# Shifting rows by DMA within SBUF instead of by matrix products, a regrouped long convolution, and a split tail, in a two-layer diffusion trunk

## The reference

```python
u = xm @ w_in                                   # 3584 columns and 16 gate columns
def short_conv3(x, w):                          # along the 128 tokens, on 1536 columns
    xp = jnp.pad(x, ((0, 0), (1, 1), (0, 0)))
    return xp[:, :L] * w[0] + xp[:, 1:L + 1] * w[1] + xp[:, 2:] * w[2]
v, x1, x2 = jnp.split(short_conv3(u[..., :1536], conv_w), 3, axis=-1)
z = x1 * (long_conv(v, h[0]) + d[0] * v)        # long_conv: by Fourier transform, length 256
z = x2 * (long_conv(z, h[1]) + d[1] * z)
...                                             # beside it: bidirectional mLSTM on q, k, v, gates
out = sum over 8 experts e of gates[:, e] * swiglu(x, w1[e], w3[e], w2[e])
x = x + g2 * out                                # the two outputs of 128 x 1024
```

## Time and profile before

| what | value |
|---|---|
| median of 3 runs | 1426.8 us (1423.72 to 1427.9) |
| the profiled execution: its own time | 1426.66 us |
| its span, first to last instruction | 1424.8 us |
| mean granted TensorE clock | 0.979 of full speed |
| busy: PE, DVE, ACT, POOL | 1352.3, 1040.3, 811.0, 29.6 us |
| the mixer's stretch with the short convolution | about 134 to 192 us |
| start of the mixer's output projection on PE | 251.87 us |
| expert stage | about 590 to 1411 us |
| last instruction of DVE | 1419.56 to 1420.25 us |

### The profile page before, as it was taken

The page is one execution under the profiler, slowest core; times in us unless marked ns, Lnnn a source line. Parts: engine busy times, 40 slices in busy tenths (PEclk is TensorE's granted clock), DMA queues, the critical chain, the costliest instruction groups (busy, mean ns, idle before and its releaser), DMA issues.

```text
span 1424.8 us, 16335 instructions
## 1 busy us (share of the span) xinstructions
PE 1352.3 (95%) x6382; PEld 1052.3 (74%) x6382; DVE 1040.3 (73%) x1008; ACT 811.0 (57%) x893; POOL 29.6 (2%) x52
## 2 busy tenths in 40 slices
PE   5889998999999988999999999999999999999994
PEld 1566564778888777788888888888888888888883
DVE  0446447754544685578898898998988988989885
ACT  1343212444334556467777777777777777777672
POOL 3000000000000200000000000000000000000000
PEclk9799999999999999999999999999999999999997
DMA  9899958765555522459999999999999999999990
GB/s 328 310 330 336 328 199 295 191 214 195 183 177 187 175 74 90 148 187 363 365 355 351 340 347 363 366 348 337 349 339 366 366 345 342 347 363 364 345 336 32
DMA packets 289348, 405.17 MB, mean 284 GB/s; under 512 B 16117, under 2 KB 224272, under 8 KB 289200
## 3 DMA queue, kind: packets, MB, share of 16 engines
q1 hardware_dynamic: 282048, 391.23, 80.4%
q0 software_dynamic: 2944, 8.47, 1.9%
q10 hardware_dynamic: 4272, 4.34, 0.9%
HBM read 402.12 MB, written 1.87 MB: 284 GB/s over the span
## 4 chain that ended last, share of the span: by engine, by line
PE 87%; DVE 5%; ACT 3%; DMA 3%; issue 1%; SPq 1%; DVEq 0%
PE bank L1773 84%; DMA raw<-in_w_ada 2%; PE bank L2140 2%; DVE w_lo L506 1%; DMA raw<-in_ev_w_in 1%; ACT arena L1044 1%; SPq L607 1%; ACT w_hi L499 1%; DVE Gb L1211 0%; PE bank L1829 0%; ACT xn L795 0%; DVE x_lo L1219 0%; PE bank L2237 0%; PE bank L2271 0%; DVE arena L1763 0%
## 5 line engine op out<-in xcount | busy, mean ns | idle before, releaser
L506 DVE TENSOR_TENSOR w_lo<-raw,w_hi 128x2048 fp32r<-128x2048 f32 (+1 forms) x238 | 543.3, 2284 | 157.2 <-ACT w_hi L499 155.5
L499 ACT CAST w_hi<-raw 128x2048 fp32r<-128x2048 f32 (+1 forms) x238 | 451.8, 1899 | 138.4 <-PE bank L1773 85.1
L1773 PE MATMUL bank<-w_hi,x_hi 128*128 128x512 f32 x1072 | 433.8, 405 | 6.3 <-DVE x_lo L1219 1.7
L1773 PE MATMUL bank<-w_lo,x_hi 128*128 128x512 f32 x1072 | 422.6, 394 | 0.0
L1773 PE MATMUL bank<-w_hi,x_lo 128*128 128x512 f32 x1072 | 419.9, 392 | 0.0
L1773 PEld LDWEIGHTS bank<-w_hi,x_hi 128*128 128x128 f32 x1072 | 202.0, 188 | 55.3 <-issue 9.5
L1773 PEld LDWEIGHTS bank<-w_hi,x_lo 128*128 128x128 f32 x1072 | 202.3, 189 | 46.5
L1773 PEld LDWEIGHTS bank<-w_lo,x_hi 128*128 128x128 f32 x1072 | 202.5, 189 | 38.6 <-issue 0.2
L506 DVE TENSOR_TENSOR w_lo<-arena,w_hi 128x2048 fp32r<-128x2048 f32 x88 | 201.7, 2292 | 36.3 <-ACT w_hi L499 36.3
L499 ACT CAST w_hi<-arena 128x2048 fp32r<-128x2048 f32 x88 | 168.0, 1910 | 28.0 <-PE bank L1773 28.0
L1773 PE MATMUL bank<-w_hi,g_hi 128*128 128x512 f32 x440 | 174.1, 396 | 1.8 <-DVE g_lo L1487 1.8
(11 more groups left out here) (281 smaller groups left out, 923.3 us busy)
## 6 DMA issues: line engine op xcount, KB each, us to landing
raw<-in_moe_w SPq DMA_DIRECT2D x352, 512.0 KB, 5.5
arena<-in_moe_w SPq DMA_DIRECT2D x176, 512.0 KB, 5.4
raw<-in_w_ada SPq DMA_DIRECT2D x96, 512.0 KB, 6.9
raw<-in_ff_w SPq DMA_DIRECT2D x66, 512.0 KB, 4.4
raw<-in_ev_w_in SPq DMA_DIRECT2D x28, 512.0 KB, 8.5
raw<-in_at_w_qkv SPq DMA_DIRECT2D x12, 512.0 KB, 4.4
raw<-in_ev_w_out SPq DMA_DIRECT2D x8, 512.0 KB, 6.3
Gb<-gate_rows POOLq DMA_DIRECT2D x8, 512.0 KB, 4.5
```

The lines of the kernel that those rows point to most:

```text
L499: nc.scalar.copy(w_hi[:, t % SPL, c], place[:, c]).then_inc(hi_ok, 1)
L506: nc.vector.tensor_tensor(w_lo[:, t % SPL, c], raw_slot(n)[0][:, c], w_hi[:, t % SPL, c].bitcast(F32), ALU.subtract).then_inc(lo_ok, 1)
L1773: return pe.matmul(out, lhsT, rhs, start=start, stop=stop)
```

## The change

- The short convolution uses no matrix products. ACT issues, for each block of 512 columns, two DMAs within SBUF: `u`'s rows 0 to 126 go to rows 1 to 127 of `earlier`, rows 1 to 127 to rows 0 to 126 of `later`, for both `g` at once. DVE's `short_conv(c)` waits until both have landed and then makes three products and two sums. POOL zeroes the two edge rows once, which it waits for ahead of its DMA of the taps.
- The mixer's order is changed on PE, ACT and DVE: all `weight_logs` come before pair 11, `fft(0)` to `inverse_fft(3)` lie between `mixer_half(11, 1)` and `ada(23)` and each comes one or two pieces earlier than before. Two blocks of the convolution's DMAs wait for `cv_ok`, in ACT's own order.
- In every expert's last chunk `down` finishes bank 4 before bank 5, with a semaphore between them, and ACT and DVE split each half by itself. The last expert's `combine` goes by halves of the columns, into four banks. POOL prepares `x` and the factor ahead of it, so that DVE makes one product and one sum for each quarter, and ACT issues four stores, each when its quarter is ready, before the flag is read.

```diff
-        ztmp = hyT0[:, 2, :]
+        ztmp = xn[:, 1, 0:HW]
+        earlier, later = hyT0[:, 0:2, :], hyT0[:, 2:4, :]
...
@@ gpsimd
+            pool.wait_ge(f_nrm, 2)
+            gp.memset(earlier[0:1], 0.0).then_inc(sh_z, 1)
+            gp.memset(later[96:P], 0.0).then_inc(sh_z, 1)
             for w in range(3):
                 if w:
                     pool.wait_ge(cv_ok, 2 * w)
...
+            pool.wait_ge(cb_t, 4 * (NE - 1))
+            last_gate = rw[:, 68:88].rearrange("p (g e) -> p g e", g=G)[:, :, NE:NE + 1]
+            for q in range(4):
+                g, c = q // 2, slice(512 * (q % 2), 512 * (q % 2) + 512)
+                chained(gp.tensor_tensor(stage[:], acc[:, g, c], Gb[:, g, c], ALU.mult))
+                chained(gp.tensor_tensor(x[:, g, c], x[:, g, c], stage[:], ALU.add))
+                chained(gp.tensor_scalar(acc[:, g, c], Gb[:, g, c], last_gate[:, g, :], None, ALU.mult))
+                pool.sem_inc(x_sum, 1)
@@ scalar
+            def shift_rows(w):
+
+                if w == 0:
+                    eng.wait_ge(sh_z, 2)
+                else:
+                    eng.wait_ge(cv_ok, 2 * w)
+                eng.wait_ge(tj_t, 7 + 2 * w + 2)
+                uw = u[:, :, HW * w:HW * w + HW]
+                eng.dma_start(earlier[1:P], uw[0:P - 1]).then_inc(sh_l, 16)
+                eng.dma_start(later[0:P - 1], uw[1:P]).then_inc(sh_l, 16)
...
             take_pair(7, block_of(u, 0))
+            shift_rows(0)
             high(IN[10])
             take_spectra(4)
             take_spectra(5)
             high(IN[11])
-            take_pair(9, block_of(u, HW))
-            high(IN[12])
             weights(0)
             weights(1)
+            take_pair(9, block_of(u, HW))
+            shift_rows(1)
+            high(IN[12])
+            weights(2)
+            weights(3)
             high(IN[13])
             take_pair(11, block_of(u, 2 * HW))
+            shift_rows(2)
             high(IN[14])
-            weights(2)
-            weights(3)
...
+            def store(r):
+
+                for i in range(2):
+                    c = slice(512 * i, 512 * i + 512)
+                    for g, name in enumerate(("y_prompt", "y_sample")):
+                        eng.wait_ge(fin, 4 * r + 2 * i + g + 1)
+                        eng.dma_start(o[name][0][:, c], x[:, g, c]).then_inc(stored, 16)
@@ vector
+            def short_conv(c):
 
                 w, g = c // 2, c % 2
+                uc, before, after = u[:, g, HW * w:HW * w + HW], earlier[:, g, :], later[:, g, :]
                 eng.wait_ge(ld_cw, 16 * (w + 1))
+                eng.wait_ge(sh_l, 32 * (w + 1))
+                v_.tensor_tensor(before, before, convw[:, 0, :], ALU.mult)
                 link(v_.tensor_tensor(uc, uc, convw[:, 1, :], ALU.mult))
+                v_.tensor_tensor(after, after, convw[:, 2, :], ALU.mult)
+                link(v_.tensor_tensor(uc, uc, before, ALU.add))
+                v_.tensor_tensor(uc, uc, after, ALU.add).then_inc(cv_ok, 1)
...
             low(IN[9])
             low(IN[10])
+            short_conv(0)
+            short_conv(1)
             low(IN[11])
             weighted(0)
             weighted(1)
+            low(IN[12])
+            short_conv(2)
+            short_conv(3)
             weighted(2)
             weighted(3)
+            low(IN[13])
...
             fft_product(0)
+            low(IN[14])
+            short_conv(4)
+            hyena_gate(0)
+            short_conv(5)
@@ tensor, from pair 9 on (new order)
             mixer_half(9, 0)
             ada(14)
             weight_logs(0)
             weight_logs(1)
             mixer_half(9, 1)
             ada(15)
+            eng.wait_ge(wt_ok, 1)
+            weight_logs(2)
+            eng.wait_ge(wt_ok, 2)
+            weight_logs(3)
             mixer_half(11, 0)
             ada(16)
             mixer_half(11, 1)
             eng.wait_ge(st_ok, 4)
+            eng.wait_ge(cv_ok, 1)
             fft(0)
+            ada(17)
+            mixer_half(13, 0)
+            inverse_fft(0)
...
+            eng.wait_ge(cv_ok, 2)
+            fft(1)
+            ada(18)
             mixer_half(13, 1)
+            inverse_fft(1)
...
             ada(19)
+            fft(2)
```

More of the change, by code:

```diff
@@ L532, in phase_of, with last_bank @@
             return 0 if m < 4 else 1 if m < 20 else 2
+        def last_bank(i, g):
+            return bank[i] if g else bank[2 + i]
         def in_bank(t):
@@ L1105, in _ @@
                 experts(1)
-            eng.wait_ge(fin, 1)
-            for g, name in enumerate(("y_prompt", "y_sample")):
-                eng.dma_start(o[name][0], x[:, g, :]).then_inc(stored, 16)
+                store(1)
         @block.vector
@@ L1423, in _ @@
             sq = hyT0[:, 0:2, :]
-            hyena_gate(0)
+            fft_product(1)
+            hyena_gate(1)
             head_rows(0)
             head_rows(1)
-            fft_product(1)
+            fft_product(2)
             head_rows(2)
@@ L1891, in spectra @@
                 mm(bank[4 + q % 2][:, :], C(("fc", "fs0", "fd")[k]), both, True, True).then_inc(f_spec, 1)
-            def conv(c):
-                eng.wait_ge(cw_ok, c + 1)
-                for i in range(2):
-                    ins = mm(bank[4 + c % 2][:, :], C("shift")[:, P * i:P * i + P], hyT0[:, 2 * (c % 2) + i, :],
-                             i == 0, i == 1)
-                ins.then_inc(cv_mm, 1)
             def weight_logs(q):
@@ L2054, in _ @@
             ada(19)
-            fft(1)
+            fft(2)
             eng.wait_ge(nu_t, 1)
@@ L2066, in _ @@
             ada_cols(1)
[L2067 removed]
+            inverse_fft(2)
             eng.wait_ge(ld_C[1], 16)
@@ L2073, in _ @@
             ada(21)
-            fft(2)
+            fft(3)
             eng.wait_ge(kw_ok, 1)
@@ L2151, in down @@
                     eng.wait_ge(gl_ok, n_unit(f, c, g))
+                    if f is not FFN0 and c % NCH == NCH - 1:
+                        for h in range(2):
+                            cc = slice(512 * h, 512 * h + 512)
+                            for j in range(2):
+                                gh, gl = (t[:, b, P * j:P * j + P] for t in (g_hi, g_lo))
+                                mm(bank[4 + h][:, :], gh, hi[:, j, cc], False, False)
+                                mm(bank[4 + h][:, :], gh, lo[:, j, cc], False, False)
+                                ins = mm(bank[4 + h][:, :], gl, hi[:, j, cc], False, j == 1)
+                            if h == 0:
+                                ins.then_inc(y_half, 1)
+                        continue
                     for j in range(2):
@@ L2350, in experts @@
                 down(f, NCHE - 1)
-                for h in range(G):
-                    combine(NE * r + NE - 1, NE - 1, h)
+                combine_last(NE * r + NE - 1)
             experts(0)
```

141 lines of the change are left out of this document (60 added, 81 removed).

## The result

The changed kernel takes 1555.7 us (median of 4, 1554.11 to 1557.72) against 1427.35 before: a ratio of 1.090 (95% interval 1.088 to 1.092), 128 us slower. The forecast was 1541, in a range of 1495 to 1585. The profiled execution took 1557.0 us.

The account below looks back on a forecast made before the run. PE's own order was taken to set the time, if DMA can follow; with one engine carrying the shifts, DMA sets the mixer's path. 1426.7 + 124 (projection later) - 10 (tail) = 1541 us, range 1495 to 1585.

Parts of the forecast that it names:

- One engine: Mixer's shift DMAs: 127 is prime, so one engine carries both of a pair, 508 packets x 80 ns = 41 us.
- the count of extra packets in the trace of before: Stores before the change: one extra packet per engine taking part; 16, 16 and 4 engines, always with equal shares of rows.
- The pairs' lives: Mixer, issue to landing of each shift pair: 41 us plus 2.7 per tile loaded meanwhile, 2.1 for taps, 1.4 to start.
- the term for what the same engine carries beside: Weight tiles, taps and states on the shifts' engine: 18 us for pair 0, 18.5 for pair 1, 13.0 for pair 2.
- DVE's waits: Mixer: DVE would wait three times for a DMA ahead of `short_conv`, some 54, 55 and 42 us.
- From `fft(1)` to the projection: Mixer's end: 37.4 us before becomes 47, with moved work, clock and numerators added, waits away, 1.6 given back; projection at 376.
- The tail: Last `down` to the end: split halves, four quarters and the flag read after the last store give 10 us.
- the 29 set as the upper bound: POOL's twelve new operations in the last expert: at most 2.4 us each, 29 us, hidden either way.
- the bound at 9: Last expert: POOL's operations holding DVE cost at most +9 us; 0 was taken.
- The first rival: Mixer's shifts: all 16 engines share the 127 rows unequally, pairs land within 8 us; 1405 us (1395 to 1415), chance 0.12.
- DMA limits the stretch; of the 4 us saved 2 are lost: Stretch up to pair 11 with spread shifts: 8.1 MB or 21.2 us of DMA against 17.9 of PE; front gives 12.
- The 14.5 us that leave PE: Mixer: three shift pairs (10.6 us) and three waits (5.5) go, 1.6 comes back at the output projection, if nothing holds the order up.

Follow-up runs that it names:

- the table of the four kernels: Changed kernel with shifts as 127 rows from ACT: 1555.7 us; 127 from POOL: 1501.5; 124 and 3 from ACT: 1456.9; 112 and 15 from ACT: 1420.5.

## Why the prediction was right, and where its terms were off

**One engine.** The step that decided, the count of extra packets in the trace of before, held: 510 packets a pair, 25 GB/s, and 135 us come back when the rows are cut so that they divide. The rows of before showed only equal shares and left the unequal one open, which the forecast kept as a rival; the counts for 124, 112, 15 and 3 rows rule it out. The packet was taken as 80 ns and measured 82.

**The pairs' lives.** Landings were forecast at 194.7, 262.5 and 324.8; DVE started at 198.1, 269.6 and 334.6. The 9.8 us are the lives of the pairs (2.0, 3.9 and 3.0 more) and 0.9 of their starts. Of each pair 1.0 us is the packet (508 x 2 ns); for the rest, 1 to 3 us a pair, the term for what the same engine carries beside was somewhat small, which is what is left over and not measured by itself.

**DVE's waits.** Forecast 54, 55 and 42 us, measured 36.0, 34.6 and 31.1. The step that failed is ACT's issue of a shift: the forecast gives it no time and lets ACT go on casting. ACT stood 21 to 25 us in the second issue of each pair, so the casts came late and DVE reached `short_conv` late (at 162.1 instead of 140.3 for the first block). It cost nothing, because it lies inside the landing time; the table of the four kernels shows that.

**From `fft(1)` to the projection.** Forecast 47 us, measured 49.7. The wait for the output tiles is 4.29 us instead of the 1.40 of before: 2.9 given back where 1.6 were forecast. So the projection starts at 388.5, not 376: 12.5 of the 16.0 us by which the profiled execution is above 1541.

**Behind the projection.** No change was forecast; it was +3.3 us in this execution. PE's timeline against that of before divides it. The first products of the output projection bring +1.1: behind the wait of 4.29 us twelve of them follow each other at 0.43 us instead of 0.23, where it was seven behind 1.40. From there to the expert stage it is +1.2, most of it ahead of the attention; the first seven experts give -0.8; beside POOL it is +1.9.

**The tail.** 9.6 us in the trace and 7.9 to 9.8 in the runs of it alone, forecast 10. POOL's twelve operations took 36.9 us of its time, above the 29 set as the upper bound (3.1 us each against 2.4), and were hidden, since 72 us were there (1473.4 to 1545.1). Their cost was put at 0, and the bound at 9; PE lost 1.9 us by them.

**The first rival was wrong in size.** The forecast gave it 1405 us if the rows were spread; spread, they give 1420.5. The failed term is "DMA limits the stretch; of the 4 us saved 2 are lost", which priced a shift byte as any other byte and PE's stop at its own length. One pair pushed out 1.52 MB of weights in place of 1.04, and PE's stops of 2.96 and 4.45 us were each followed by products at half clock. The 14.5 us that leave PE are near what the run without DMAs shows at the projection (12.3); in the medians 8 to 9 remain of it, and the DMAs take more than that.

Still open: how the 10.7 us of the spread DMAs divide between the number of DMAs, their bytes and the clock beyond the two steps above, and why the attention's products run at half clock in one execution and not in another, which takes 3.4 us of the lead at the projection.

## What to carry to other kernels

Count the engines of a DMA before using it on a path: look at the slowest dimension of the rows, and where 16 doesn't divide it (127, 124) cut it into a part that 16 divides and a rest. Then ask which resource the stretch has to spare: replacing PE's work by DMAs gained nothing where DMA was full, although the front without the DMAs was worth 8 to 9 us. For the block where DMA's share was 0.6 it cost nothing, and a gain of its own isn't shown. And price a stop of PE with the half clock behind it, not only with its length.

## What the runs showed of the hardware that was not expected

- The engine that issues a DMA can be held: 21 to 25 us in the second issue of a pair of 508 KB on one DMA engine, 8.9 to 10.4 us in the third of four with 4 engines, 0.6 to 1.9 us with 16. From POOL's software queue an issue of 127 rows took 3.6 us with one engine, and one of 112 or 15 rows 0.6 to 0.7 us.
- POOL's queue gave two successive DMAs of one engine each to different engines (50 GB/s together); ACT's gave both to the same (25 GB/s). With 127 rows POOL's queue carried 12288 packets more than before, 2048 for each of the six DMAs, most of them under 512 bytes, where ACT's carried 255 a DMA.
- Copies within SBUF beside full weight loads: 98 to 99 ns for a packet of 2 KB in both queues, against 84 with weight loads alone and 82 on a lone engine.
- POOL's operations on 128 x 512 float32, beside a busy DVE, took 1.3 to 2.2 us (product), 3.2 (sum) and 3.5 to 5.6 (scaling by a column), where DVE's take 0.7; beside them DVE's subtraction of 128 x 2048 grew from 2.29 to as much as 3.38.
